# Paged decoder layer: each value page goes into 64 partitions, two tokens to a row of 4 KB

## The chip, the cores and the metric

The kernel runs on one core of a Trainium2 chip. The metric is the device time of one execution in microseconds (us); the median over runs is compared.

## The reference, cut to what matters

One layer of a hybrid decoder: adaLN and RMSNorm, one input projection, two token mixers side by side (block-sparse softmax attention over a paged cache, and gated linear attention, GLA), their merge, and a mixture of 32 experts. All is float32. There are 512 prompt tokens and 8 sequences (samples) with 4 new tokens and 2048 past tokens each. The past tokens lie in pages of 128 tokens, 16 pages to a sequence, found through a page table:

```python
k_past = cache_k[layer, pages].reshape(past_len, A_HEADS, A_HEAD_DIM)   # 2048 x 8 x 64
v_past = cache_v[layer, pages].reshape(past_len, A_HEADS, A_HEAD_DIM)
...
p = jax.nn.softmax(logits, axis=-1)
out = jnp.einsum('hqnk,hqnkd->hqd', p_sel, v_sel) + jnp.einsum('hqk,hkd->hqd', p_own, v_own)
```

A token has 512 floats of value (8 heads by 64), 2 KB. A page has 256 KB. There are 128 pages of keys and 128 of values.

## The kernel before

**The ring.** Everything large is loaded into a ring of 6 slots of 2 MB (128 partitions by 16 KB). The list `stream` holds the blocks in order; `SLOT_ORDER` gives the slot of each. Around the change the order is: modulation weights, the three projection weights for q, k and v, 16 blocks of key pages, 16 blocks of value pages, then the GLA weights. A block may be loaded when the block that was in its slot has been used; for a value block that is counted by the semaphore `pv_s`. The value blocks go round five slots, so at most five are loaded or on their way while one is used.

**Who issues.** A page block has 8 pages, one DMA each. SP's queue issues pages q = 0, 2, 4, 6 (`load_pages` with `range(0, 8, 2)`, line 467), GpSimd's queue pages 1, 3, 5, 7 (line 587). Both go through their blocks in the order of `stream`: SP has 64 key pages and 64 value pages, and so has GpSimd. Behind the value pages SP's queue carries the GLA weights. Between its key pages GpSimd also issues eight loads of the table of position biases (line 596), each 128 KB from an internal DRAM buffer of 192 KB into 16 partitions.

**Where a page lies.** Page q of a block lies in columns 512 q to 512 q + 511 of the slot, token t in partition t. This holds for keys and values. A value block holds two neighbouring pages (2i, 2i + 1) of each of four sequences: q = 4 (page % 2) + j for sequence j of the group. So 8 blocks serve four sequences (group g = 0), the next 8 the other four.

**Who uses it.** VectorE turns a key block in 32x32 pieces (line 1158), TensorE makes scores of it, and after 8 blocks of keys the softmax of a group of four sequences can run. Its weights lie in `logits[g]`, 128 rows (sequence, head, query) by 2048 tokens. `weights_turned` (group 0) and `later_weights_turned` (group 1) turn them with TensorE, 128 tokens at a time, so that tokens lie in partitions; ScalarE copies them out. `page_values(v)` then waits for the value block (`landed`: SP's and GpSimd's halves both) and does 16 matmuls: two pages by four sequences by, for each, its 32 columns of weights against 512 columns of values, in float32 that accumulate over all pages of the group in one PSUM bank.

**The order on TensorE** is written out by hand. The loop over z = 1 to 18 (line 1933) puts together the prompt's attention (scores, turned weights, products of the unit z) and one value block for each z up to 16: `page_values(z - 1)`. At z = 2 to 6 `later_weights_turned` stands before `page_values`, so that the value block 1 and all that follow stand behind the second softmax, which needs the last key block. After the loop come the GLA projections.

Of the kernel before, what the change touches and what calls it, by code (L numbers as in the profile page):

```python
# [13 lines left out]
P = 128  # L14
# [11 lines left out]
AW = AH * AD  # L26
# [82 lines left out]
def layer_kernel(nc, x_prompt, x_sample, c_prompt, c_sample, cache_k, cache_v, state_gla, page_table,  # L109
# [4 lines left out]
    with ExitStack() as ctx:  # L114
# [36 lines left out]
        ps = ctx.enter_context(nc.psum_tensor("ps", [P, 8, 512], F32))  # L151
# [25 lines left out]
        def s(name):  # L177
            if name not in S:
                S[name] = sem(name)
            return S[name]  # L180
# [7 lines left out]
        SLOT_ORDER = ([3, 4, 1, 2, 0, 5, 3] + [4, 1, 2, 0, 4, 1, 2, 0, 4, 1, 5, 2, 0, 4, 1, 5] + [2, 0, 3, 4, 1] * 3 + [2]  # L188
                      + [0, 3, 4, 1, 2, 5] * 2 + [0, 3, 4, 1] + [2, 5, 3, 4, 1, 2, 0, 5] + [3, 4])
# [10 lines left out]
        def slot(n):  # L200
            return ring[:, SLOT_ORDER[n], :]
# [9 lines left out]
        def block(used, *parts):  # L211

            n = len(stream)
            return add_block([columns(w, lo, n, cols, at, k) for w, lo, cols, at, k in parts], len(parts), used)
# [17 lines left out]
        for h in range(GH):  # L232
            a = block((s("v_ps"), 2 * h + 2), (w_in[0], OFF["qg"] + GDK * h, GDK, 0, KD), (w_in[0], OFF["kg"] + GDK * h, GDK, KD * GDK, KD),
                      (w_in[0], OFF["vg"] + GDV * h, GDV, 2 * KD * GDK, KD))
# [74 lines left out]
        logits, o_rows = [logit0, logit1], [logit0[:, 0:AW], logit1[:, 0:AW]]  # L309
# [20 lines left out]
        def page_weights(g, page):  # L330

            if g == 0:
                return prT[:, page, :]
            return (prT_low, prT_high)[page // 8][:, page % 8, :]
# [16 lines left out]
        def key_sequence(k):  # L351
            return 4 * (k // 8) + k % 4
# [87 lines left out]
        def load_pages(eng, n, pieces, which, sems):  # L440

            what, i = pieces
            cache = cache_k if what == "k" else cache_v
            for q in which:
                pg = 8 * i + q
                if what == "k":
                    at = key_sequence(i) * PAGES + 8 * (i // 4 % 2) + q
                else:
                    at = (4 * (pg // (4 * PAGES)) + pg % 4) * PAGES + pg // 4 % PAGES
                page = eng.value_load(ptab[0:1, at:at + 1], min_val=0, max_val=cache.shape[1] - 1)  # L450
                src = cache[0, bass.DynSlice(page, 1)].rearrange("a t h d -> (a t) (h d)")
                eng.dma_start(slot(n)[:, AW * q:AW * q + AW], src).then_inc(sems[SLOT_ORDER[n]], 16)  # L452


        @blk.sync
# [1217 lines left out]
        def _(pe):  # L1673
            def mm(out, lhsT, rhs, start, stop, **k):
                return pe.matmul(out, lhsT, rhs, start=start, stop=stop, **k)  # L1675
# [8 lines left out]
            def turn(out, v):  # L1684
                n = v.shape[0]
                return pe.transpose(out, v, ident[0:n, 0:n])  # L1686
# [58 lines left out]
            for k in range(KD):  # L1745
                last = turn(ps[:, 5, 9 * k:9 * k + 9], crow[:, 1, P * k:P * k + P])
# [76 lines left out]
            def keys_folded(f):  # L1823

                pe.wait_ge(s("key_rows"), 4 * f + 4)
                if f:
                    pe.wait_ge(s("sc_taken"), 2 * f)
                else:
                    pe.wait_ge(*after("own_taken"))
                    pe.wait_ge(s("key_fold_in"), 16)  # L1830
                for x in range(2):
                    out = ps[:, (3, 7)[x], :].rearrange("p (g i b) -> p i g b", g=4, i=4)
                    for i in range(4):
                        for j in range(4):
                            last = mm(out[32 * j:32 * j + 32, i], key_fold[:, 32 * i:32 * i + 32], key_rows[f % 2][:, j, P * x:P * x + P], True, True,
                                      skip_group_check=True)
                last.then_inc(s("fold_ps"), 1)
# [35 lines left out]
            scores(0)  # L1873
            keys_folded(3)

            def weights_turned():
                pe.wait_ge(s("l_norm"), 1)
                for q in range(5):
                    if q >= 2:
                        pe.wait_ge(s("pr_T"), q - 1)  # L1880
                    if q == 4:
                        last = turn(ps[0:NS, 7, 0:P], logits[0][:, PAST:])
                    else:
                        for page in range(4 * q, 4 * q + 4):
                            last = turn(ps[:, (6, 1)[q % 2], P * (page % 4):P * (page % 4) + P], logits[0][:, P * page:P * page + P])
                    last.then_inc(s("pr_tr"), 1)

            def later_weights_turned(q):
                pe.wait_ge(s("l_norm"), 2)
                pe.wait_ge(s("pr_T"), 5 + q)  # L1890
                if q >= 2:
                    pe.wait_ge(s("p_ov"), q - 1)
                if q == 4:
                    last = turn(ps[0:NS, 1, 0:P], logits[1][:, PAST:])
                else:
                    for page in range(4 * q, 4 * q + 4):
                        last = turn(ps[:, 1, P * (page % 4):P * (page % 4) + P], logits[1][:, P * page:P * page + P])
                last.then_inc(s("pr_tr"), 1)

            def page_values(v):  # L1900
                g, i = v // (PAGES // 2), v % (PAGES // 2)
                if i == 0:
                    pe.wait_ge(s("pr_T"), 5 * g + 5)
                    if g:
                        pe.wait_ge(s("o_rows"), g)
                    for j in range(4):
                        mm(ps[32 * j:32 * j + 32, 0, :], pr_own[0:NS, 32 * j:32 * j + 32], v_tok[0:NS, PT, :], True, False,
                           skip_group_check=True)
                n = PAGED[("v", v)]
                landed(pe, n)  # L1910
                for page in (2 * i, 2 * i + 1):
                    for j in range(4):
                        q = 4 * (page % 2) + j
                        last = mm(ps[32 * j:32 * j + 32, 0, :], page_weights(g, page)[:, 32 * j:32 * j + 32], slot(n)[:, AW * q:AW * q + AW],
                                  False, page == PAGES - 1, skip_group_check=True)
                last.then_inc(s("pv_s"), 1)
# [16 lines left out]
            for z in range(1, UNITS + 3):  # L1933
# [6 lines left out]
                if z <= PAGES:  # L1940
                    page_values(z - 1)
                if 2 <= z <= UNITS + 1:
# [3 lines left out]
                    for o in range(2):  # L1946
                        pe.wait_ge(s("p_norm"), 2 * y + o + 1)
                        for j in range(y % PT + 1):
                            last = turn(ps[:, 6 + o, P * j:P * j + P], sc_p[:, y % 3, o, P * j:P * j + P])
                    last.then_inc(s("p_tr"), 1)  # L1950
                if z >= 3:
                    y = z - 3
                    p, i = y // PT, y % PT
# [7 lines left out]
                    for j in range(i + 1):  # L1961
                        for o in range(2):
                            h = 2 * p + o
                            last = mm(ps[64 * o:64 * o + 64, 1, 0:P], v_tok[:, j, AD * h:AD * h + AD],
                                      pt_p[:, y % 2, o, P * j:P * j + P], j == 0, j == i, skip_group_check=True)
                    last.then_inc(s("p_pv"), 1)
            for half in range(2):
                for k in range(KD):
                    r = slice(32 * (k % 4), 32 * (k % 4) + 32)
                    last = mm(ps[r, 4 + half, 0:HALF], wgk[:, k, :], hT[:, k, HALF * half:HALF * half + HALF], k < 4, k >= 4,  # L1970
                              skip_group_check=True)
# [50 lines left out]
            for h in range(GH):  # L2022
# [32 lines left out]
                for j in range(4):  # L2055
                    last = mm(ps[NS * j:NS * j + NS, 7, 0:P], e_end[:, sample], ident, True, True, skip_group_check=True)
# [12 lines left out]
                for i in range(PT):  # L2069
                    t0, n = P * i, place_of[i]  # L2070
# [16 lines left out]
                    for c in range(CPT):  # L2087
                        r = slice(CHUNK * c, CHUNK * c + CHUNK)
                        last = mm(ps[:, 4 + c, 0:GDV], kend[r, i, :], v_g[r, i, :], True, True)
# [6 lines left out]
                    if i == 1:  # L2096
# [6 lines left out]
                        for r in range(2):  # L2103
                            for j in range(4):
                                b = 4 * r + j
                                last = mm(ps[NS * j:NS * j + NS, 0, 0:GDV], q_mask[:, NS * b:NS * b + NS], state_s[:, b, :], False, r == 1,
                                          skip_group_check=True)
# [5 lines left out]
                    if i >= 2:  # L2113
# [3 lines left out]
                        for j in range(4):  # L2117
                            rows = slice(NS * j, NS * j + NS)
                            last = mm(ps[:, 4 + j, 0:GDV], kend_m[rows, i - 2, :], v_g[rows, 4, :], True, True)
# [8 lines left out]
                    for c in range(CPT):  # L2128
                        at = CPT * i + c
# [3 lines left out]
                        r = slice(CHUNK * c, CHUNK * c + CHUNK)  # L2133
# [6 lines left out]
            for t in range(KD):  # L2140
                n = MERGE[t]
# [24 lines left out]
            for q in range(2):  # L2166
                for k in range(KD):
                    if q == 0:
                        pe.wait_ge(s("merged"), k + 1)
                    r = slice(NS * (k % 4), NS * (k % 4) + NS)  # L2170
                    last = mm(ps[r, 4 + q, :], mergedT[:, k, sample], w_half[q][:, k, :], k < 4, k >= 4, skip_group_check=True)
            last.then_inc(*done("parts_ps"))
            pe.wait_ge(s("router_in"), 32)
            for k in range(KD):
                last = mm(ps[0:64, 7, 288:297], wr[:, k, :], mod[:, 3, k, :], k == 0, k == KD - 1)
# [176 lines left out]
            for i in range(PT):  # L2352
                pe.wait_ge(s("y_gated"), i + 1)
                for half in range(2):
                    last = mm(ps[:, 2 * i + half, :], ident, ya[i][:, 512 * half:512 * half + 512], False, True)
# [27 lines left out]
```

## Time and profile before

| | us |
|---|---|
| median of 3 runs | 1369.53 (1369.01 to 1375.62) |
| the profiled execution, its own time | 1372.72 |
| the profiled execution, first to last instruction (span) | 1371.0 |
| TensorE busy | 1225.5 (89%) |
| VectorE, ScalarE, GpSimd busy | 384.1, 235.7, 189.4 |
| all DMA | 372.59 MB, mean 272 GB/s |

How to read it: the profile is of one execution. The page cuts the span into 40 slices of 34.3 us and gives for each the busy share of an engine in tenths (9 is 90% or more) and the rate of the DMA engines. The keys and values are loaded in slices 2 to 7 (counted from 0). The long stretch of the second half is the experts' weights. L12 is line 12 of the kernel; nearly all matmuls have line 1675 and nearly all turns by TensorE line 1686, where the two helpers stand. "SPq" is SP's queue of instructions, "POOL" GpSimd. In the rows of DMA queues q1 is what SP issues and q0 what GpSimd issues.

### The profile page before, as it was taken

The page shows a single profiled execution, that of the slowest core. Times are in us where ns is not written, and L with a number is a line of the kernel's source. Part 1 is how long each engine was busy: PE and PEld are TensorE (multiplying, and loading weights), DVE is VectorE, ACT ScalarE, POOL GpSimd, SP SyncE. Part 2 cuts the span into 40 slices and gives each one's busy share as a digit, 9 for nine tenths or more (in the row PEclk, how much of TensorE's full clock was granted, in tenths as well). Part 3 has the DMA queues.
Part 4 walks back from the last instruction along what each step waited for, and adds up shares of the span by engine and source line. Part 5 has one row for each costly group of instructions (what it writes and reads, how often), then busy time and mean ns, then how long its engine had stood idle before and what let it go on. Part 6 is the DMA issues. An engine that isn't in the chain of part 4 may idle for free.

```text
span 1371.0 us, 17800 instructions
## 1 busy us (share of the span) xinstructions
PE 1225.5 (89%) x6825; PEld 692.9 (51%) x6825; DVE 384.1 (28%) x764; ACT 235.7 (17%) x514; POOL 189.4 (14%) x282
## 2 busy tenths in 40 slices
PE   4999959899999999999999997998887888877976
PEld 2344434375767676788888555343333333322432
DVE  3479866521323233200000225311111001010104
ACT  3121234322323232100000122000000000000002
POOL 2323423200101011100000001101011000010000
PEclk9999989999999999999999998899999999999998
DMA  9969998972645542552104626899999999999975
GB/s 352 363 220 319 321 388 315 372 312 62 245 159 175 126 120 55 158 146 77 62 0 160 254 31 182 327 404 423 424 423 422 427 425 424 424 422 424 424 306 199
DMA packets 116152, 372.59 MB, mean 272 GB/s; under 512 B 10948, under 2 KB 56533, under 8 KB 96622
## 3 DMA queue, kind: packets, MB, share of 16 engines
q1 hardware_dynamic: 93664, 308.96, 58.7%
q0 software_dynamic: 19280, 55.49, 11.9%
q10 hardware_dynamic: 3134, 7.16, 1.7%
q8 instruction: 46, 0.75, 0.2%
q14 instruction: 28, 0.23, 0.0%
HBM read 359.29 MB, written 22.36 MB: 278 GB/s over the span
## 4 chain that ended last, share of the span: by engine, by line
PE 65%; DMA 25%; DVE 4%; SPq 3%; ACT 2%; issue 2%; POOL 0%; ACTq 0%; POOLq 0%; DVEq 0%
PE ps L1675 62%; DMA ring<-in_w_exp_up 20%; PE ps L1686 2%; DMA ring<-in_cache_k 2%; DMA ring<-in_cache_v 1%; SPq L450 1%; SPq L452 1%; DMA work<-in_x_prompt 1%; DVE work L1370 1%; DMA h_rows<-ring 1%; DVE work L1664 0%; SPq L476 0%; DVE work L1669 0%; DVE ring L1158 0%; ACT hx L698 0%
## 5 line engine op out<-in xcount | busy, mean ns | idle before, releaser
L1675 PE MATMUL ps<-ring,work 128*64 128x512 f32 (+3 forms) x1952 | 448.5, 597 | 70.1 <-DMA ring<-in_w_exp_up 48.2
L1675 PEld LDWEIGHTS ps<-ring,work 128*64 128x64 f32 (+2 forms) x1952 | 159.9, 144 | 323.4 <-issue 269.8
L1675 PE MATMUL ps<-ring,hx 128*32 128x256 f32 (+3 forms) x1584 | 275.4, 449 | 16.6 <-DVE ring L1158 7.3
L1675 PEld LDWEIGHTS ps<-ring,hx 128*32 128x32 f32 (+1 forms) x1584 | 158.9, 147 | 115.5 <-issue 79.1
L1675 PE MATMUL ps<-hx,ring 128*128 128x272 f32 x768 | 180.7, 395 | 0.6 <-DVE work L1370 0.6
L1675 PEld LDWEIGHTS ps<-hx,ring 128*128 128x128 f32 x768 | 146.3, 191 | 31.8 <-DVE work L1370 1.1
L1675 PE MATMUL ps<-work,ring 128*128 128x272 f32 (+2 forms) x464 | 97.7, 369 | 0.7 <-ACT ring L990 0.7
L1629 DVE TENSOR_TENSOR work<-work,ps 128x256 f32<-128x256 f32 x32 | 13.5, 421 | 280.4 <-ACT work L1028 280.4
L1675 PEld LDWEIGHTS ps<-work,ring 128*128 128x128 f32 (+1 forms) x464 | 81.4, 188 | 18.6 <-issue 2.7
L1686 PE MATMUL ps<-cst,work 128*128 128x128 f32 (+4 forms) x349 | 65.6, 306 | 27.4 <-DMA work<-in_norm_g 7.7
L1028 ACT ACTIVATE work<-ps 128x256 f32<-128x256 f32 x32 | 12.3, 384 | 434.7 <-PE ps L1675 434.7
L1675 PE MATMUL ps<-work 32*128 32x256 f32 (+13 forms) x690 | 72.9, 376 | 10.8 <-DVE work L1097 6.1
L1686 PEld LDWEIGHTS ps<-cst,work 128*128 128x128 f32 (+4 forms) x349 | 48.9, 183 | 60.1 <-issue 35.5
L1158 DVE STREAM_TRANSPOSE ring<-ring 128x4096 f32<-128x4096 f32 x16 | 71.1, 4441 | 22.0 <-DMA ring<-in_cache_k 22.0
L648 POOL DMA_INDIRECT expert_rows<-work x32 | 32.0, 1000 | 326.2 <-DVE work L1635 316.2
L1404 DVE TENSOR_TENSOR work<-work,ps 128x544 f32<-128x544 f32 x16 | 11.5, 722 | 193.7 <-PE ps L1675 193.7
L1675 PEld LDWEIGHTS ps<-work 32*128 32x128 f32 (+6 forms) x690 | 36.9, 161 | 39.7 <-issue 29.8
L1635 DVE COPY work<-ps 128x512 f32<-128x512 f32 x32 | 22.1, 692 | 123.4 <-PE ps L1675 123.4
L452 POOL DMA_DIRECT2D ring<-in_cache_k x64 | 34.4, 538 | 75.6 <-issue 74.9
L452 POOL DMA_DIRECT2D ring<-in_cache_v x64 | 34.8, 544 | 63.1 <-issue 61.0
L609 POOL TENSOR_TENSOR work<-work,ong 128x256 f32<-128x256 f32 x20 | 14.3, 724 | 176.0 <-ACT work L919 176.0
L631 POOL TENSOR_TENSOR work<-work 128x544 f32<-128x544 f32 x8 | 10.7, 1334 | 184.0 <-DVE work L1404 184.0
(306 smaller groups left out, 761.4 us busy)
## 6 DMA issues: line engine op xcount, KB each, us to landing
ring<-in_w_exp_down SPq DMA_DIRECT2D x32, 2048.0 KB, 22.6
ring<-in_w_exp_gate SPq DMA_DIRECT2D x31, 2048.0 KB, 17.8
ring<-in_w_exp_up SPq DMA_DIRECT2D x31, 2048.0 KB, 22.2
ring<-in_w_ada SPq DMA_DIRECT2D x12, 2048.0 KB, 23.0
ring<-in_cache_k SPq DMA_DIRECT2D x64, 256.0 KB, 9.5
ring<-in_cache_k POOLq DMA_DIRECT2D x64, 256.0 KB, 6.5
ring<-in_cache_v SPq DMA_DIRECT2D x64, 256.0 KB, 11.1
ring<-in_cache_v POOLq DMA_DIRECT2D x64, 256.0 KB, 6.5
```

Source lines behind the costliest of these rows:

```text
L450: page = eng.value_load(ptab[0:1, at:at + 1], min_val=0, max_val=cache.shape[1] - 1)
L452: eng.dma_start(slot(n)[:, AW * q:AW * q + AW], src).then_inc(sems[SLOT_ORDER[n]], 16)
L609: pool.tensor_tensor(v, v, ong[:, :], ALU.mult).then_inc(s("og_ready"), 1)
L648: pool.indirect_dma_start(y_dram[:, :], bass.IndirectOffsetOnAxis(ap=index, axis=0), ye[r], None, bounds_check=2 * NT * 2 - 1, oob_is_err= ...
L1028: act.activation(hid[par], ps[:, 2 + par, 0:256], ACT.Silu).then_inc(s("hid_gate"), 1)
L1158: dve.transpose(slot(n), slot(n)).then_inc(s("page_tr"), 1)
L1370: dve.scalar_tensor_tensor(state_s[:, b, :], state_s[:, b, :], decay[:, NCH + b:NCH + b + 1], ps[:, 4 + b % 4, 0:GDV], ALU.mult, ALU.add). ...
L1404: dve.tensor_tensor(halves(v[:, t % 2, :]), halves(v[:, t % 2, :]), wide(w), ALU.mult).then_inc(s("m_scaled"), 1)
L1629: dve.tensor_tensor(hid[par], hid[par], ps[:, 2 + par, 256:512], ALU.mult).then_inc(s("hid"), 1)
L1635: dve.tensor_copy(ye[r], ps[:, 4 + par, :]).then_inc(s("ye_ready"), 1)
L1675: return pe.matmul(out, lhsT, rhs, start=start, stop=stop, **k)
L1686: return pe.transpose(out, v, ident[0:n, 0:n])
```

## The change

Value pages are stored otherwise in their slot. Where a page lay in 128 partitions with one token (2 KB) in each, it now lies in 64 partitions with two tokens, 2p and 2p + 1, side by side in a row of 4 KB. Pages 0 to 3 of a block (the even pages of the four sequences) go to partitions 0 to 63, pages 4 to 7 (the odd ones) to partitions 64 to 127; page q and page q + 4 have the same columns, 1024 (q % 4) to 1024 (q % 4) + 1023. A slot is as full as before. Who issues which page, in which order and behind which wait, stays.

A column block of 512 now holds, over its 128 partitions, the tokens of one parity of two neighbouring pages. So the weights have to be turned for these: `every_other` takes every second of 256 columns in place of 128 dense ones. The matmuls of `page_values` take the column block 2 j + page % 2. Their number and sizes stay. Key pages don't change.

```diff
@@ load_pages
-                src = cache[0, bass.DynSlice(page, 1)].rearrange("a t h d -> (a t) (h d)")
-                eng.dma_start(slot(n)[:, AW * q:AW * q + AW], src).then_inc(sems[SLOT_ORDER[n]], 16)
+                if what == "k":
+                    src = cache[0, bass.DynSlice(page, 1)].rearrange("a t h d -> (a t) (h d)")
+                    eng.dma_start(slot(n)[:, AW * q:AW * q + AW], src).then_inc(sems[SLOT_ORDER[n]], 16)
+                else:
+                    src = cache[0, bass.DynSlice(page, 1)].rearrange("a (p u) h d -> (a p) (u h d)", u=2)
+                    r, j = 64 * (q // 4), q % 4
+                    eng.dma_start(slot(n)[r:r + 64, 2 * AW * j:2 * AW * j + 2 * AW], src).then_inc(sems[SLOT_ORDER[n]], 16)
@@ TensorE
+            def every_other(v, page):
+
+                at = 2 * P * (page // 2) + page % 2
+                return v[:, at:2 * P * (page // 2) + 2 * P:2]
+
@@ weights_turned
-                            last = turn(ps[:, (6, 1)[q % 2], P * (page % 4):P * (page % 4) + P], logits[0][:, P * page:P * page + P])
+                            last = turn(ps[:, (6, 1)[q % 2], P * (page % 4):P * (page % 4) + P], every_other(logits[0], page))
@@ later_weights_turned
-                        last = turn(ps[:, 1, P * (page % 4):P * (page % 4) + P], logits[1][:, P * page:P * page + P])
+                        last = turn(ps[:, 1, P * (page % 4):P * (page % 4) + P], every_other(logits[1], page))
@@ page_values
-                        q = 4 * (page % 2) + j
+                        q = 2 * j + page % 2
```

## Rows read from the trace of the kernel before

**Rows 1.** The page: busy by engine, the 40 slices, GpSimd's issues.
```profile
PE 1225.5 (89%) x6825; PEld 692.9 (51%) x6825; DVE 384.1 (28%) x764; ACT 235.7 (17%) x514; POOL 189.4 (14%) x282
...
DMA  9969998972645542552104626899999999999975
GB/s 352 363 220 319 321 388 315 372 312 62 245 159 175 126 120 55 158 146 77 62 0 160 254 31 182 327 404 423 424 423 422 427 425 424 424 422 424 424 306 199
...
L452 POOL DMA_DIRECT2D ring<-in_cache_v x64 | 34.8, 544 | 63.1 <-issue 61.0
```

**Rows 2.** The chain that ended last, 150 to 340 us: start, us, what.
```profile
158.87 21.58 DMA ring<-in_cache_k
180.47 4.46 DVE ring L1158
...
246.43 18.16 DMA ring<-in_cache_v
264.64 1.92 PE ps L1675 x16
```

**Rows 3.** Waits of TensorE, 190 to 320 us: in total, times, longest.
```profile
PE ps L1686 <- DVE work L1222: 6.0, 1, 6.0
PE ps L1675 <- DMA ring<-in_cache_v: 5.3, 3, 3.3
```

**Rows 4.** TensorE's timeline, 190 to 320 us: start, us, what, idle before it.
```profile
206.15 3.35 PE L1675 MATMUL ps<-ring 128*32 128x512 f32 x16
...
211.45 1.92 PE L1675 MATMUL ps<-ring 128*32 128x512 f32 x16
...
258.73 1.92 PE L1675 MATMUL ps<-ring,hx 128*32 128x512 f32 x16 [3.33 <-DMA ring<-in_cache_v]
...
271.75 1.92 PE L1675 MATMUL ps<-ring,hx 128*32 128x512 f32 x16
...
284.40 16.49 PE L1675 MATMUL ps<-hx,ring 128*128 128x272 f32 x64
```

**Rows 5.** Stretches: busy time of each engine, granted clock, DMA share, GB/s last.
```profile
156.50:160.50 4.00, 4.00 (x20) 1.56 (x23) 4.00 (x1) 0.77 (x3) 2.09 (x4) 1.00 1.05 381
161.00:163.50 2.50, 1.90 (x40) 1.07 (x36) 0.00 (x0) 0.38 (x1) 0.57 (x2) 1.00 1.07 215
164.50:167.00 2.50, 2.50 (x7) 1.06 (x7) 2.50 (x1) 0.25 (x1) 1.28 (x3) 1.00 1.04 391
167.00:169.50 2.50, 2.50 (x8) 1.06 (x7) 2.46 (x3) 0.00 (x0) 1.01 (x2) 1.00 1.05 205
...
180.00:185.00 5.00, 0.03 (x4) 0.03 (x5) 4.45 (x1) 0.37 (x1) 2.14 (x4) 0.50 1.03 386
...
246.00:262.00 16.00, 11.96 (x108) 5.28 (x104) 7.75 (x19) 4.95 (x15) 6.42 (x12) 1.00 1.04 386
960.00:1300.00 340.00, 281.81 (x1264) 108.65 (x1262) 34.64 (x71) 21.60 (x44) 32.48 (x32) 0.94 1.01 424
```

**Rows 6.** DMA queues, 162 to 180 us: packets, MB, share of 16 engines.
```profile
q0 software_dynamic: 1206, 3.93, 64.5%
q1 hardware_dynamic: 1204, 2.19, 37.9%
```

**Rows 7.** DMA issues, 246 to 262 us: KB each, median us to landing.
```profile
ring<-in_cache_v POOLq DMA_DIRECT2D x12, 256.0 KB, 6.4
ring<-in_cache_v SPq DMA_DIRECT2D x9, 256.0 KB, 14.4
```

**Rows 8.** The same of 155.4 to 155.6 us, then of 160.5 to 160.7.
```profile
work<-bias_rows POOLq DMA_DIRECT2D x1, 128.0 KB, 9.2
...
work<-bias_rows POOLq DMA_DIRECT2D x1, 128.0 KB, 10.2
```

**Rows 9.** Weight loads of line 1686, 875 to 925 us, then 189 to 225.
```profile
L1686 PEld LDWEIGHTS ps<-cst,work x22: 186/194/303, 881.7 to 920.5; 128*128 128x128 f32 x22
...
L1686 PEld LDWEIGHTS ps<-cst,hx x20: 138/140/143, 209.4 to 222.5; 128*128 128x128 f32 x20
```

## The prediction, made before the changed kernel ran

> **What bounds the kernel now.** I read the page first [rows 1]. TensorE is busy for 89% of the span, but the DMA rows say where it isn't the whole story: slices 5 to 8 of 40 (137 to 274 us), which hold the last key pages and all the value pages, have the DMA engines full (digit 9, except one 8). So I went to the chain that ended last for that stretch [rows 2]. It has to be read from the top. Until 180.47 it is a transfer: the last page block of keys lands then. From there comes one chain of dependent steps: VectorE turns the keys, TensorE scores them, the second softmax follows, and TensorE turns its weights. Only behind that, in program order, stands the second value block, at 206.15 [rows 4]. Later the chain is a value transfer again, 246.43 to 264.64, and behind it TensorE work to the end of the stage.
>
> How large are these waits? TensorE waited 5.3 us for value pages in three pieces, and 6.0 us for the second softmax [rows 3]. The longest piece stands before the block at 258.73, and the last block starts at 271.75 [rows 4]. Behind the stage nothing makes up time: TensorE runs on into the GLA projections at 284.40 [rows 4].
>
> Then the transfers themselves. SP has 64 value pages and GpSimd 64, each 256 KB: 33.55 MB. At the full rate of 386 GB/s [rows 5] that is 87 us, in a stage that lasts 102 from the first page's issue (162.5) to the end of the last such wait (264.6). The slack is small, and part of it is spent in the wait for slots (315 GB/s in slice 7, from 206 to 240 us [rows 1]). So this stage lives on the transfer rate, and two questions decide: what do 4 KB rows do to the rate, and what does it do to write to 64 partitions only.
>
> **The change part by part.** *Rows of 4 KB.* In 162 to 180 the two queues moved nearly the same number of packets, 1206 and 1204, but 3.93 MB and 2.19 MB [rows 6]. So GpSimd's queue already moves about 4 KB in a packet and SP's about 2 KB, and the engines take a packet from each in turn. With 4 KB rows SP's packets of values grow, GpSimd's don't. That has two effects. First, less overhead: the rate with rows of 8 and 16 KB is 424 GB/s against 386 [rows 5], so 4 KB on one of two queues can be worth between 0 and 10% of the transfer; 3% (2.6 us of 87) is my estimate, since half the bytes are in such packets already. Second, evenness: pages issued by SP in 246 to 262 land 14.4 us after issue, GpSimd's 6.4 us [rows 7], and a block needs both. With equal packets both would land near the mean, some 10 us, so SP's half comes up to 4 us earlier. Together these can remove the 5.3 us of waits and hardly more, because TensorE's own work from 206.15 on is then the bound. The last key block gains nothing: its pages keep 2 KB packets beside GpSimd's 4 KB.
>
> *64 partitions.* No transfer of before does this at length, so I looked for the nearest and found the eight bias loads of line 596, 128 KB into 16 partitions each. One is issued at 155.5 and lands 9.2 us later, one at 160.6 and lands after 10.2 us [rows 8]. The rate around them [rows 5]: 381 GB/s in 156.5 to 160.5, 215 in 161 to 163.5, 391 behind it, 205 in 167 to 169.5, with the DMA engines as busy as ever (1.04 to 1.07). A dip of 2.5 us from 386 to 210 GB/s costs 0.44 MB of transfer. So 0.128 MB to an eighth of the partitions took the time of 0.57 MB, over four times its size, and the packets of both queues suffered. Either the narrow destination does it, or the source (1 KB pieces of one small buffer); before can't tell the two apart. If it is the destination, each half of the partitions takes half of the full rate, and a page in 64 partitions costs twice its size at most: nothing extra when the other queue is writing the other half at the time, double when both write the same half. I take the destination as the likelier reason.
>
> Here the Trainium skill speaks against the change. SBUF — State Buffer, section Door 1: The DMA port swizzle (why `[64,N]` ≈ `[32,N]`), says that partitions 0 to 63 are reached through 8 of the 16 ports, and gives 196 GB/s for 64 partitions against 328 for 128 at 1 MiB, a factor of 1.67; its 16 partitions reach four ports, and with the dip above the trace agrees. By that factor on every value page the sum below would be 42 us instead of 27.6, by an estimate from that page.
>
> Which halves meet? Each block of 8 pages goes q = 0, 2, 4, 6 on SP and 1, 3, 5, 7 on GpSimd: two pages to the lower half, then two to the upper, on both. If the queues are in step they always hit the same half. If they are two pages apart, never; at a random offset half the time. A queue that is alone (the other waiting for a slot, or SP's queue still holding keys) always doubles. Average cost of a value page f: between 1 and 2; I take 1.5.
>
> *The sum.* At 162 some 2.5 MB of keys are still to come (SP's queue moved 2.19 MB in packets up to 180 [rows 6]; the rest is GpSimd's last page). Keys and values at f need (2.5 + 33.55 f) MB / 386 GB/s: 93 us for f = 1, 137 us for 1.5, 180 us for 2. From 162.5 this ends at 256, 299.4 and 343. Today the last block starts at 271.75, so f = 1.5 moves it by 27.6 us, f = 2 by 71, and up to f = 1.18 the stage would fit. All of that passes to the end, as nothing behind waits for anything else.
>
> *The key tail.* While GpSimd's values run beside SP's last keys, a round of one packet each costs 2 + 4 KB now and 2 + 8 KB at the double price: 1.67 times. The 17.5 us up to 180.47 would grow by 0 to 11.7 us. It lies inside the sum above as long as transfers bound the stage; where they don't (f near 1.2 and below), it moves 206.15 on, and 11.7 − 5.3 = 6.4 us is what remains.
>
> *The rest costs nothing.* GpSimd needs 544 ns for the issue of a page [rows 1], and fewer rows may shorten that by something between nothing and all; but what waits is the transfer, which is behind the issue by 6 to 14 us [rows 7], so that neither end changes the sum. The weights are now turned from every second column. Turns with a step of 8 floats need 194 ns for the load of the weights against 140 for dense ones [rows 9], and the load lies beside the matmul of the turn before. From below it costs nothing, from above 32 turns by 54 ns, 1.7 us; I take nothing, since the step here is 2 floats and the engine waits for transfers anyway. The value products only take another column block, and each block's 16 matmuls stay at 1.92 us. When TensorE waits for pages its granted clock drops to 0.50 of full speed, the 1.2 GHz level (180 to 185, after the wait for the last keys [rows 5]), and the 16 products took 3.35 us at 206.15 against 1.92 [rows 4]; beside a transfer this is covered, uncovered it costs 1.4 us once or twice.
>
> **The rivals.**
> A, my forecast: half of the pages' time is doubled. +10 us at f = 1.3, +27.6 at 1.5, +45 at 1.7.
> B, 64 partitions cost nothing; the dips came from the bias loads' source. Then only the larger packets act: the waits of 5.3 us go, 1364 to 1368. For it speaks that the source of those loads is unusual too; it is decided for B if the rate of the value stage is at or above 386 GB/s.
> C, no overlap of the halves at all, f = 1.8 to 2: +54 to +71. The skill's page also says, under "Can I just issue two DMAs to hit both halves?", that two transfers to the two halves ran only 6% faster than one; no row here shows it.
> D, the queues happen to run two pages apart: f below 1.25. Then key tail and lost waits nearly cancel, 0 to +6.4 us.
> That the transfers are covered anyway is excluded by [rows 2, 3]. B ends on the other side of A.
>
> **How the numbers follow.** The profiled execution took 1372.72 us (span 1371.0); the median of the runs is 1369.53, 3.2 less, while 1.7 of the profiled time lies outside the span. A: 1372.7 + 27.6 − 3.2 = 1397. Chances: A 0.45, B 0.25, C 0.12, D 0.18. 0.5% is 6.8 us, about what a measurement tells from no change: 1362.7 to 1376.4 is the same. A and C are slower, D for 0.04: 0.61. B is mostly inside the bound (0.20) and so is the rest of D (0.14): 0.34. For faster B must give more than the waits: 0.05. A's own range is 1380 to 1415. The range for all reaches from B's 1364 to f = 1.77, 1425; it leaves out most of C and a bit of B.
>
> **What the profile after would show.** For A: the rate in the value stage falls well below 386 GB/s with the DMA engines still at 1.0; in stretches where one queue moves values alone it is near half. Value pages on both queues take longer to land, the last key block lands after 180.47, TensorE's wait for value pages grows from 5.3 to over 25 us in many pieces, the granted clock shows it. SP's queue has 4096 packets fewer (64 pages by 64 rows), GpSimd's as many. Wrong I'd be if the rate stays; then the packet counts and the landing times of the two queues (nearly equal) show B. If the last value block starts before 272 with a rate below 386, slots and not transfers were the bound.

## The result: 3.5% slower

The changed kernel takes 1421.29 us (median of 4 runs), the kernel before 1372.16 in the same comparison; the ratio is 1.0351, interval 1.0324 to 1.0378. The forecast of 1397 was 24 us short of it, in a range of 1364 to 1425; forecast A's own range ended at 1415. The profiled execution took 1421.10 us, its span is 1419.4, which is 48.4 more than before.

The page of the changed kernel, its slices and its queues:
```profile
DMA  9979999998264543265110733699999999999974
GB/s 356 335 256 325 301 294 227 223 214 331 60 236 154 191 100 115 53 179 129 60 60 0 301 114 89 210 407 424 423 424 425 425 422 425 425 422 424 422 327 192
...
q1 hardware_dynamic: 89568, 308.96, 58.6%
q0 software_dynamic: 19280, 55.49, 13.6%
```
SP's queue in the kernel before:
```profile
q1 hardware_dynamic: 93664, 308.96, 58.7%
```
Slices 6 to 8 (counted from 0) stand at 227, 223 and 214 GB/s, and the digits of the DMA engines there are 9. SP's queue (q1) has 89568 packets, 4096 fewer than before, and GpSimd's (q0) has 19280 as before. The change did what it says: SP's value rows are 4 KB now.

The chain of the changed kernel from 150 to 400 us, which answers to [rows 2]:
```profile
156.97 28.23 DMA ring<-in_cache_k
185.22 4.46 DVE ring L1163
...
238.79 32.81 DMA ring<-in_cache_v
271.65 3.41 PE ps L1680 x16
279.50 39.68 DMA ring<-in_cache_v
319.23 3.46 PE ps L1680 x16
```
Its waits of TensorE from 190 to 340 us, which answer to [rows 3]:
```profile
PE ps L1680 <- DMA ring<-in_cache_v: 35.4, 10, 6.1
...
PE ps L1691 <- DVE work L1227: 6.0, 1, 6.0
```
And its timeline, which answers to [rows 4]:
```profile
210.65 3.14 PE L1680 MATMUL ps<-ring 128*32 128x512 f32 x16
...
243.48 3.64 PE L1680 MATMUL ps<-ring 128*32 128x512 f32 x16 [6.11 <-DMA ring<-in_cache_v]
...
319.23 3.46 PE L1680 MATMUL ps<-ring,hx 128*32 128x512 f32 x16 [5.93 <-DMA ring<-in_cache_v]
...
333.69 11.49 PE L1680 MATMUL ps<-hx,ring 128*128 128x272 f32 x44
```
Read the four starts against rows 4: the second value block is 4.5 us late, the last 47.5, the GLA projections 49.3, and the end of the kernel 48.4. So 4.5 us were lost in the key tail, 43 in the value blocks, and nothing behind them gave any back. Of the 43, 30.1 show as waits for pages (35.4 against 5.3). The other 12.9 are TensorE's own time for the same work at a lower granted clock, from the start of the second value block to that of the last, before and then after:
```profile
206.15:271.75 65.60, 59.65 (x496) 25.88 (x495) 37.47 (x89) 26.61 (x72) 21.57 (x40) 0.98 0.96 344
```
```profile
210.65:319.23 108.58, 72.54 (x497) 30.14 (x496) 39.72 (x94) 29.05 (x76) 20.71 (x40) 0.81 1.05 223
```
TensorE is busy for 72.5 us where it was for 59.7, at a granted clock of 0.81 against 0.98; the 16 products at 243.48 took 3.64 us where they take 1.92 at full clock. I don't count that part as a second cause: the DMA engines are full in this stretch (1.05), so with faster products the same transfer would have been waited for longer. No run tests that by itself.

The rates, stretch by stretch (columns as in rows 5), in the changed kernel:
```profile
216.00:218.00 2.00, 2.00 (x19) 0.59 (x12) 1.93 (x4) 0.69 (x2) 0.92 (x2) 1.00 1.07 236
222.00:262.00 40.00, 28.89 (x219) 13.43 (x217) 16.52 (x40) 12.33 (x32) 13.45 (x26) 0.86 1.05 224
262.00:310.00 48.00, 29.58 (x178) 11.50 (x178) 14.14 (x33) 8.82 (x24) 4.20 (x8) 0.76 1.05 222
```
and in the kernel before, for the same stretch:
```profile
222.00:262.00 40.00, 35.51 (x313) 16.46 (x313) 21.91 (x53) 15.32 (x44) 16.72 (x31) 1.00 1.04 385
```
The DMA engines are as busy with 224 GB/s (1.05) as with 385 (1.04). The stretch at 216 to 218 is one in which GpSimd's queue was nearly empty. Its queues:
```profile
q1 hardware_dynamic: 135, 0.45, 101.4%
q8 instruction: 1, 0.02, 4.2%
q0 software_dynamic: 8, 0.00, 1.2%
```
SP's queue alone fills the engines at 0.45 MB in 2 us. So one queue alone is as slow as two together (225 GB/s against 224). From 205.5 to 208 SP's values ran beside ScalarE's store of the prompt's values (q10, which reads from SBUF):
```profile
q1 hardware_dynamic: 166, 0.54, 63.4%
q10 hardware_dynamic: 170, 0.35, 37.1%
```
The values again move at 216 GB/s (0.54 MB in 2.5 us), and 140 GB/s of stores go on beside them. The values take 63% of the engines' time there where they took 101% at 216 to 218, at nearly the same rate. So I read that what is full is not the engines as such but the way into half of the partitions; the kernel with every second partition, below, tests it. Last, how late pages land when issued from 246 to 262 us, against [rows 7]:
```profile
ring<-in_cache_v SPq DMA_DIRECT2D x8, 256.0 KB, 34.9
ring<-in_cache_v POOLq DMA_DIRECT2D x8, 256.0 KB, 35.2
```
Both queues are equally late here, as equal packets should make them; but both at 35 us.

### The profile page after: what moved, and what is told of

Its sections match the earlier page's. It is cut to its first block, busy times and chain, and to the rows that moved or that the text cites. A ratio compares the mean times of both kernels' runs of the same rounds, so it can differ in the third digit from the quotient of the medians.

```text
span 1419.4 us, 17800 instructions
## 1 busy us (share of the span) xinstructions
PE 1240.2 (87%) x6825; PEld 699.2 (49%) x6825; DVE 384.8 (27%) x764; ACT 235.8 (17%) x514; POOL 188.2 (13%) x282
## 3 DMA queue, kind: packets, MB, share of 16 engines
q1 hardware_dynamic: 89568, 308.96, 58.6%
q0 software_dynamic: 19280, 55.49, 13.6%
## 4 chain that ended last, share of the span: by engine, by line
PE 63%; DMA 28%; DVE 3%; SPq 3%; ACT 2%; issue 1%; POOL 0%; ACTq 0%; POOLq 0%; DVEq 0%
PE ps L1680 60%; DMA ring<-in_w_exp_up 19%; DMA ring<-in_cache_v 5%; PE ps L1691 2%; DMA ring<-in_cache_k 2%; SPq L450 1%; SPq L457 1%; DMA work<-in_x_prompt 1%; DMA work<-expert_rows 1%; DVE work L1375 1%; SPq L481 0%; DVE ring L1163 0%; ACT hx L703 0%; SPq L548 0%; DMA work<-h_rows,idx 0%
## 5 line engine op out<-in xcount | busy, mean ns | idle before, releaser
L1680 PE MATMUL ps<-ring,work 128*64 128x512 f32 (+3 forms) x1952 | 455.5, 611 | 79.9 <-DMA ring<-in_w_exp_up 47.4
L653 POOL DMA_INDIRECT expert_rows<-work x32 | 32.0, 1000 | 324.2 <-DVE work L1640 319.2
```

What stands on the lines that cost most here:

```text
L653: pool.indirect_dma_start(y_dram[:, :], bass.IndirectOffsetOnAxis(ap=index, axis=0), ye[r], None, bounds_check=2 * NT * 2 - 1, oob_is_err= ...
```

## The experiments

All times are medians, compared with the kernel before on the same chip. In the diffs of this part the ends of lines (`.then_inc(...)`) are left out, and "..." stands for lines that are cut.

**Whose half, and when.** Four kernels keep the 64 neighbouring partitions and change only who writes which half at what time. First GpSimd's order turned round:

```diff
-                load_pages(pool, n, (what, i), range(1, 8, 2), page_sem)
+                load_pages(pool, n, (what, i), range(1, 8, 2) if what == "k" else (5, 7, 1, 3), page_sem)
```


> The changed kernel with GpSimd's value pages issued in the order 5, 7, 1, 3, so that GpSimd writes the upper 64 partitions while SP writes the lower ones and the reverse. Theory H (each half of the partitions takes half of the full rate, and the two queues run in step in the same half): the rate in the value stage rises from 222 GB/s to 380 or more wherever both queues hold values two pages apart, about 1372 to 1385 us; a stretch in which one queue is alone stays near 220. Rival R1 (rows of 4 KB, or DMAs of 64 rows, are slow by themselves wherever they go) and rival R2 (what counts is the number of partitions of a DMA, whatever the other queue does): 222 GB/s and 1421 us, nothing changed.

It took 1417.97 us, ratio 1.0341 (1.0301 to 1.0382). Its rate:
```profile
222.00:262.00 40.00, 30.24 (x207) 13.13 (x205) 15.92 (x38) 11.01 (x29) 12.21 (x25) 0.83 1.04 231
```
A miss for theory H as I had put it: 231 GB/s, 3% above the changed kernel, and 1418 us in place of 1372 to 1385. The Trainium skill, SBUF — State Buffer, section "Can I just issue two DMAs to hit both halves?", gives a gain of 6% for two transfers to the two halves. The 3% of this run are near it, as far as the queues were in opposite halves at all. For issue order is not arrival order, so I let each queue have its own half for good:

```diff
-                    load_pages(sp, n, pieces, range(0, 8, 2), slot_sem)
+                    load_pages(sp, n, pieces, range(0, 8, 2) if pieces[0] == "k" else range(0, 4), slot_sem)
...
-                load_pages(pool, n, (what, i), range(1, 8, 2), page_sem)
+                load_pages(pool, n, (what, i), range(1, 8, 2) if what == "k" else range(4, 8), page_sem)
```


> The changed kernel with SP issuing pages 0 to 3 of every value block (always the lower 64 partitions) and GpSimd pages 4 to 7 (always the upper ones). H: the queues can't meet in one half, whatever their lag, so 380 to 410 GB/s whenever both hold values; SP's packets are 4 KB too, so both halves of a block land about equally late; 1366 to 1380 us. It could be the best form if the time in which one queue is alone is short. R1 and R2: 222 GB/s and 1421 us.

1394.83 us, ratio 1.0144 (1.0111 to 1.0177). Rate:
```profile
222.00:262.00 40.00, 36.11 (x297) 16.29 (x297) 21.87 (x52) 16.49 (x46) 16.43 (x32) 0.96 1.04 289
262.00:290.00 28.00, 18.23 (x147) 7.63 (x144) 11.41 (x29) 8.21 (x21) 2.18 (x4) 0.94 1.04 303
```
So the halves matter, with the same DMAs in the same numbers: 303 against 222 GB/s. But 303 isn't 386, and 1395 isn't 1366 to 1380: two queues in opposite halves overlap only in part. By the 6% of the Trainium skill, in the section named above, they should hardly overlap. Here the rate is 29 to 36% above 224 and 222, and the measurement decides.

Then two orders one page apart, which were to use the lag seen in the first:

```diff
+                load_pages(pool, n, (what, i), range(1, 8, 2) if what == "k" else (5, 1, 3, 7), page_sem)
```


> The changed kernel with GpSimd's value pages issued in the order 5, 1, 3, 7 (upper, lower, lower, upper; SP still lower, lower, upper, upper). Issuing two pages apart gave only 231 GB/s, and in the last blocks there GpSimd's pages landed about one page ahead of SP's. H, with the lag between the queues counted: if GpSimd is one page ahead again, both queues are in the same half throughout, 220 to 225 GB/s, about 1421 us; if it is not ahead, they share a half for two pages of four, about 255 GB/s and 1407 us. Rival R3 (two queues never overlap in the two halves as long as each changes its half page by page; only a queue that stays in its own half gains): 220 to 235 GB/s here and in the next one alike.

```diff
+                load_pages(pool, n, (what, i), range(1, 8, 2) if what == "k" else (1, 5, 7, 3), page_sem)
```


> As the one before, with the order 1, 5, 7, 3 (lower, upper, upper, lower). H with the lag counted: if GpSimd is one page ahead, the queues are in opposite halves throughout, 300 GB/s as in the kernel where each queue has its own half, about 1395 us; if it is not, about 255 GB/s and 1407 us. R3: 220 to 235 GB/s, 1412 to 1421 us.

1418.92 us (1.0355, 1.0334 to 1.0375) and 1416.24 us (1.0316, 1.0287 to 1.0345). The rates of the first, then of the second:
```profile
222.00:262.00 40.00, 29.00 (x217) 12.74 (x215) 16.15 (x39) 11.74 (x30) 12.91 (x26) 0.87 1.04 251
```
```profile
222.00:262.00 40.00, 29.77 (x227) 12.45 (x223) 18.19 (x44) 14.04 (x38) 13.96 (x27) 0.87 1.04 252
```
Both reach about 251 GB/s, as expected for a shared half in two pages of four, and above the 220 to 235 of R3; so R3 is out by the rate, and the fixed lag of one page that I had assumed isn't there. The times, expected at 1407, are a miss: 12% more rate than the changed kernel, and 2 to 5 us of time by the medians. In the profiled execution of the first (1415.79, its fastest) the last value block does start 7.1 us earlier than in the changed kernel, at 312.17. In that of the second (1420.87, its slowest) it starts at 321.76, later than the 319.23 of the changed kernel. Here is why, for that execution. Four pages that SP issued one behind the other, and the one after them, with their time to landing:
```profile
ring<-in_cache_v SPq DMA_DIRECT2D x1, 256.0 KB, 25.5
ring<-in_cache_v SPq DMA_DIRECT2D x1, 256.0 KB, 26.5
ring<-in_cache_v SPq DMA_DIRECT2D x1, 256.0 KB, 27.5
ring<-in_cache_v SPq DMA_DIRECT2D x1, 256.0 KB, 38.4
ring<-in_cache_v SPq DMA_DIRECT2D x1, 256.0 KB, 23.6
```
(issued at 264.0, 265.1, 266.5, 267.9 and 274.2.) Such landings have to be read with care. SP's four pages of a block count on one semaphore, 16 for each page, and the profile takes the 16th, 32nd, 48th and 64th count as the landings of the four. Only the last, at 306.3, says that all four are there. The first page of the next block has its 16 counts at 297.8; and the packed trace has 59 of that block's 64 counts before 306.3. So most of the transfer was a block ahead, and the little that was missing held the block up. At the end of the stage the DMA engines are no longer full (0.57):
```profile
310.00:321.70 11.70, 8.37 (x46) 3.33 (x45) 3.62 (x8) 2.50 (x6) 0.00 (x0) 0.65 0.57 114
```
In the changed kernel 24 counts of the next block come before that block's last one, in the kernel with own halves 10. I read the 59 as one or two of the 16 DMA engines that had fallen behind; the counts don't name the engine.

**Rows of 4 KB, or where they go.** The same 64 partitions with rows of 2 KB (tokens p and p + 64 in a partition; the order of the weights isn't adapted, so other tokens are paired):

```diff
-                    src = cache[0, bass.DynSlice(page, 1)].rearrange("a (p u) h d -> (a p) (u h d)", u=2)
+                    src = cache[0, bass.DynSlice(page, 1)].rearrange("a (u p) h d -> (a p) u (h d)", u=2)
...
-                    eng.dma_start(slot(n)[r:r + 64, 2 * AW * j:2 * AW * j + 2 * AW], src)
+                    eng.dma_start(slot(n)[r:r + 64, 2 * AW * j:2 * AW * j + 2 * AW].rearrange("p (u c) -> p u c", u=2), src)
```


> The changed kernel with the two tokens of a partition 64 apart in place of neighbours, so that a page still lies in 64 partitions but is read in rows of 2 KB. The weights keep the order of the changed kernel, so the value sums pair other tokens; the amount of work is the same. R1, if 4 KB rows are slow: back to 386 GB/s and 1372 us. H: still slow, 1395 to 1421 us; SP's packets are then 2 KB beside GpSimd's 4 KB, so the queues may run out of step for part of the stage and the rate may lie between 222 and 386. R2: 222 GB/s, 1421 us.

1423.6 us, ratio 1.0380 (1.0360 to 1.0399); the queues from 222 to 262 us:
```profile
q0 software_dynamic: 1474, 4.79, 53.3%
q1 hardware_dynamic: 2436, 4.44, 51.6%
```
9.2 MB in 40 us, 232 GB/s. SP's packets are small again and the stage is as slow, so it isn't the rows of 4 KB (R1). The time lies just above the 1395 to 1421 that I expected.

And the DMAs unchanged, 64 rows of 4 KB, but in every second partition (weights again not adapted):

```diff
-                    r, j = 64 * (q // 4), q % 4
-                    eng.dma_start(slot(n)[r:r + 64, 2 * AW * j:2 * AW * j + 2 * AW], src)
+                    r, j = q // 4, q % 4
+                    eng.dma_start(slot(n)[r:P:2, 2 * AW * j:2 * AW * j + 2 * AW], src)
```


> The changed kernel with a value page in every second partition (even pages in the even, odd pages in the odd ones) in place of the lower or upper 64; the DMAs keep 64 rows of 4 KB. The weights keep the order of the changed kernel, so the value sums pair other tokens; the amount of work is the same. H, if it is the half that counts: each DMA reaches both halves, so the full rate of 386 to 410 GB/s even when the queues are in step or alone, the last key block lands no later than 180, 1365 to 1373 us. R1 (rows) and R2 (number of partitions): 222 GB/s and 1421 us. It tells H from R2.

1365.14 us, ratio 0.9942 (0.9923 to 0.9962). Rate and landing from 222 to 262 us:
```profile
222.00:262.00 40.00, 39.55 (x353) 18.24 (x351) 24.86 (x60) 17.04 (x46) 15.76 (x30) 1.00 1.03 408
```
```profile
ring<-in_cache_v POOLq DMA_DIRECT2D x30, 256.0 KB, 6.9
ring<-in_cache_v SPq DMA_DIRECT2D x30, 256.0 KB, 6.7
```
This decides it. Number of partitions, row size, order and queues are those of the changed kernel; only which 64 partitions differs, and 224 GB/s become 408. R2 is out, and with it the rest of R1, as these are DMAs of 64 rows of 4 KB too. It also shows what the larger packets are worth when nothing stands in their way: 408 against the 385 of the kernel before, and SP's pages land as early as GpSimd's.

**The turns.** All of the change but its loads (the value sums then pair other tokens):

```diff
-                if what == "k":
...
+                src = cache[0, bass.DynSlice(page, 1)].rearrange("a t h d -> (a t) (h d)")
+                eng.dma_start(slot(n)[:, AW * q:AW * q + AW], src).then_inc(sems[SLOT_ORDER[n]], 16)
```


> The changed kernel with its value loads put back to one page in 128 partitions; only the turns from every second column stay (the value sums then pair other tokens; the amount of work is the same). The turns cost nothing to speak of: 1371 to 1373 us, the same as before, the loads of the weights of these turns between 140 and 194 ns. If they carried part of the loss: above 1375.

1370.42 us, ratio 0.9994 (0.9982 to 1.0007): no difference from before. The load of the weights of these turns takes 209 ns, above the 194 that I had named as an end (kernel with the turns alone, 189 to 225 us):
```profile
L1686 PEld LDWEIGHTS ps<-cst,work x34: 94/209/226, 189.4 to 223.1; 128*128 128x128 f32 x32, 128*32 128x32 f32 x2
```
The time shows that it costs nothing all the same.

**The bias loads, on which the forecast rested.** Their source replaced in the kernel before; the prompt's near biases are then wrong:

```diff
-                    src = bass.AP(tensor=bias_dram.tensor, offset=P - 1 - COPIES * a, ap=[[TAB - 1, COPIES], [COPIES * TAB, AH], [1, 2 * P]])
-                    pool.dma_start(near[COPIES * a:COPIES * a + COPIES], src)
+                    src = cache_v[0, a, 0:64].rearrange("(p u) h d -> p u (h d)", u=4)
+                    pool.dma_start(near[COPIES * a:COPIES * a + COPIES].rearrange("p h c -> p (h c)").rearrange("p (u c) -> p u c", u=4), src)
```


> The kernel before with the source of the eight bias loads replaced: 64 tokens of a value page, read in rows of 2 KB from aligned places, into the same 16 partitions, 128 KB as before (the prompt's position biases near the diagonal are then wrong; the amount of work is the same). The narrow destination as the cause of the dips: the rate still falls from 386 to some 210 GB/s for about 2.5 us after each. The source as the cause: no dip, 380 GB/s or more throughout.

There is one execution, of 1368.98 us; what counts here are its rates.
```profile
160.00:162.50 2.50, 1.91 (x40) 0.96 (x36) 1.12 (x1) 0.74 (x2) 0.81 (x2) 1.00 1.08 251
163.50:166.00 2.50, 2.50 (x17) 1.13 (x10) 1.96 (x1) 0.38 (x1) 1.07 (x2) 1.00 1.04 389
166.00:168.50 2.50, 2.50 (x8) 1.06 (x7) 2.50 (x2) 0.00 (x0) 1.07 (x2) 1.00 1.08 223
```
The dips stay, at 251 and 223 GB/s against 215 and 205 in [rows 5], with 389 between them. The narrow destination makes nearly all of them. Whether the source adds the small rest, two stretches of one execution can't tell.

**A version that beats both.** The experiments ask for pages in every second partition (loads as in the run with them, and column blocks 2 j + page % 2, both left out of the diff) with weights in the matching order. ScalarE already copies the logits from PSUM, so the copy can write them in that order, and TensorE turns dense columns again:

```diff
+                    for b in (0, BLK):
+                        dst = logits[f // 2][:, at + b:at + b + BLK].rearrange("p (u t a) -> p a t u", u=2, a=2)
+                        last = act.activation(dst, ps[:, (3, 7)[x], b:b + BLK].rearrange("p (a t u) -> p a t u", a=2, u=2), ACT.Copy)
+                    last.then_inc(s("sc_taken"), 1)
...
+                last_two = logit[:, PAST - BLK:PAST].rearrange("p (u t a) -> p a t u", u=2, a=2)
+                near_part = last_two[:, 1]
```


> Pages in every second partition, rows of 4 KB, with the weights in the matching order: ScalarE writes the logits of each 256 keys in the order (token parity, token pair, page), so that TensorE turns 128 dense columns as in the kernel before, and the near bias is added through the same order. ScalarE has two copies of 256 columns where it had one of 512; that adds under 1 us to the path to the second softmax. H: the full rate of 400 to 410 GB/s as in the kernel with every second partition, no wait for value pages worth mentioning, 1364 to 1368 us, 0.4 to 0.6% faster than before. Rival (its gain came from the wrong pairing of weights): 1372 us or slower.

1365.69 us, ratio 0.9965 (0.9952 to 0.9978). Then the bias loads spread as well:

```diff
-                    src = bass.AP(tensor=bias_dram.tensor, offset=P - 1 - COPIES * a, ap=[[TAB - 1, COPIES], [COPIES * TAB, AH], [1, 2 * P]])
-                    pool.dma_start(near[COPIES * a:COPIES * a + COPIES], src)
+                    src = bass.AP(tensor=bias_dram.tensor, offset=P - 1 - a, ap=[[TAB - 8, COPIES], [COPIES * TAB, AH], [1, 2 * P]])
+                    pool.dma_start(near[a:P:8], src)
```


> The kernel with pages in every second partition and the right weights, and the eight bias loads also spread: 16 partitions eight apart in place of 16 neighbours, the same bytes from the same buffer. If where the partitions lie sets the rate, the dips after each load (205 to 215 GB/s for 2.5 us) get smaller or go, the last keys land up to 5 us earlier, and the time is 1360 to 1365 us. If the number of partitions does, the dips stay and the time is 1365.7.

1358.91 us, ratio 0.9911 (0.9891 to 0.9930), below the 1360 to 1365 that I expected. Stretches of the kernel without the spread loads, then with them:
```profile
112.00:160.00 48.00, 46.81 (x431) 23.48 (x429) 43.69 (x38) 14.50 (x27) 20.01 (x37) 1.00 1.04 338
162.00:180.00 18.00, 13.31 (x160) 6.93 (x149) 11.97 (x5) 3.66 (x8) 8.40 (x15) 0.98 1.04 374
```
```profile
112.00:160.00 48.00, 46.81 (x424) 23.62 (x426) 44.40 (x38) 14.42 (x27) 20.32 (x38) 1.00 1.02 351
162.00:180.00 18.00, 16.56 (x216) 9.13 (x212) 11.57 (x6) 4.05 (x9) 9.21 (x16) 1.00 1.03 394
```
The keys flow faster while the bias loads run, by 4% in the first stretch; there the two kernels without the spread loads differ by 2% between themselves (331 GB/s in the kernel before, 338 here), so the time is the better witness: 1365.7 to 1358.9, with intervals of the ratios that don't meet. In its chain the second value block starts at 197.87 us; it was 203.66 without the spread loads and 206.15 in rows 4. The spread loads also read the buffer with another step from partition to partition, so this run alone doesn't separate destination and source.

## Why the prediction was right, and where it was too small

*What bounds the stage.* Right: keys, softmax and value transfers in that order, and every microsecond of them passed to the end (47.5 at the last block, 48.4 at the end).

*The destination, not the source.* Right, and now shown by the replaced source and by every second partition. It was drawn from eight loads of 128 KB in a trace that has no page in 64 partitions. The Trainium skill, SBUF — State Buffer, section Door 1: The DMA port swizzle (why `[64,N]` ≈ `[32,N]`), gives 196 GB/s for 64 partitions and 328 for 128, a factor of 1.67. By an estimate from that page the last block would start 42 us later. The trace agrees in the main: 47.5 us, and rates of 385 and 224 GB/s, a factor of 1.72.

*The mean cost f of a page.* This is the term that was mis-sized. I took 1.5; from the last block's start it was (156.7 us × 386 GB/s − 2.5 MB) / 33.55 MB = 1.73, and 386 / 222 gives 1.74. So nearly every page paid the full price of a half, where I had let half of the pages pay it, and the median moved by 49.1 us where I had 27.6. Two parts of its working failed. The mean over offsets was too low, for it assumed that two queues in opposite halves lose nothing and that any offset is as likely. In the changed kernel the queues ran in step: SP's part of the ninth and the tenth value block is complete at 252.8 and 262.1 us, GpSimd's at 251.3 and 261.0. And an offset would have helped little: with two pages of distance in the issue the rate was 231, and with their own halves for good they reach 303 and not 386. The upper end of 2 was too high: a half takes 222 GB/s, more than half of 386. In part that is because 386 is itself held down by SP's 2 KB packets (408 without them); but 222 is more than half of 408 too, and why stays open. The range held by its width: 1421 is above A's own 1380 to 1415. Its upper end was also put wrongly, as f = 1.77 gives 1421 by the sum there, and 1425 belongs to 1.82. Rival C's name fits what happened better, nearly no overlap, though its price of +54 to +71 did not come; 49 did.

*The key tail.* 0 to 11.7 us were given, 4.5 came.

*The larger packets.* Rival B's mechanism is real and its size right: without the loss by the halves, the kernels with every second partition have 408 GB/s, nearly equal landing times (6.7 and 6.9 us) and 0.8 and 1.3 us of waits for value pages in place of 5.3, at 0.3 to 0.6% under before. The rate rose by 6%, where the prediction's estimate was 3%.

*The clock.* The waits lowered it as forecast (0.86 and 0.76 in the two long stretches), beside the transfer. *The turns* cost nothing; only the end of 194 ns was too low.

What stays open: how two queues in opposite halves share the way, that is, why fixed halves give 303 and alternating ones 231 to 252. The counts of the semaphores show parts of the transfer a block apart in one kernel, 52 to 59 counts of 64 in SP's blocks from the ninth on, but in the other kernels with alternating halves no more than 24 there, so this doesn't explain the rates; and no view names a single engine.

## What to carry to other kernels

The rate of a load depends on which partitions it writes, not only on row size and bytes: put 64 rows into every second partition, not into 64 neighbours (408 against 224 GB/s here), and try to spread small loads likewise. To price a form that a trace doesn't show, look for the nearest form that it does show, even in small loads, and look at what the rate does beside it. Larger rows help the queue whose packets were small, and by that the half of a buffer that used to land last.

## What the runs showed of the hardware

Loads into 64 neighbouring partitions move 222 to 236 GB/s, from one queue or two in step; 231 to 252 when the halves of the two queues alternate otherwise, 289 to 303 when each queue keeps its own half; into every second partition 408. A store goes on beside them (140 GB/s beside 216). A load of 128 KB into sixteen neighbouring partitions lowers the rate to 205 to 215 GB/s for 2.5 us; with the loads eight apart, the stretch from 112 to 160 us rises from 338 to 351 GB/s. While SP's and GpSimd's queues both have pages waiting, the engines take as many packets of the one as of the other (1204 and 1206 in rows 6), and GpSimd's packets hold 4 KB where SP's hold a row of 2 KB, so with rows of 2 KB SP's pages land later (14.4 against 6.4 us). The rate of a long stretch can rise (252 against 224 GB/s) while the last block is complete no earlier (321.7 against 319.2 us), when parts of the transfer run a block apart.
